# The experts' sum takes in the residual on TensorE, and the last norm reads PSUM

## The chip, the cores and the metric

One core of a Trainium2 chip runs the whole program in one launch. The metric is the device time of that launch in microseconds (us), the median of several runs. Everything is float32; products on TensorE (PE) are either full float32, which the trace shows as two passes per product, or products of rounded halves (fp32r) in one pass each.

## The reference, cut to what matters

Two blocks of two layers each work on 256 tokens of 1024 columns. The change is in the second block, at the end of each of its layers: the experts' output is added to the residual `h`, and after the last layer comes a last norm.

```python
def expert_choice_ffn(xn, w_router, w_gate, w_up, w_down):
    aff = softmax(xn @ w_router)                      # 256 x 16
    g, idx = top_k(aff.T, 32)                         # 32 tokens for each of 16 experts
    xs = xn[idx]
    hid = silu(xs @ w_gate[e]) * (xs @ w_up[e])
    y = (hid @ w_down[e]) * g
    return zeros_like(xn).at[idx].add(y)

for l in range(2):
    xn = rms_norm_2(h, attn_norm[l])
    ...                                               # three kinds of attention
    h = h + o @ w_out[l]
    h = h + expert_choice_ffn(rms_norm_2(h, ffn_norm[l]), ...)
return rms_norm_2(h, final_norm)                      # x * rsqrt(mean(x*x) + eps) * gain
```

## The kernel before, in words

Each engine has a function of its own (`tensor`, `vector`, `scalar`, `pool`, `sync`), and the program is what these functions issue in the order in which they are written. Nothing is scheduled: what orders engines among each other are semaphores, counted by name (`P("scat", l, q)` is PE's count, `V` VectorE's, `A` ScalarE's, `G` GpSimd's, `D` the DMAs').

The residual `x` has 128 partitions and two halves `t` of tokens by two halves `h` of columns, so four tiles of 128x512, numbered n = 2t + h. `xG` is a copy of it that ScalarE makes before the experts (`x_apart`), with the columns in another order: column 4q + c lies at c * 128 + q, so that weights loaded from it lie side by side. Who reads it back in the order of `x` steps over 512 bytes from one value to the next. The place of `x` itself is then used for expert weights.

`experts(l)` in each engine's function runs 18 stages. In stage s PE makes gate and up of expert s (`gate_up`), adds the output of expert s - 2 to the sum over experts (`scatter`: four products of 128x512, one for each tile n, which gather over all 16 experts in four PSUM banks called "moe"), makes the down product of expert s - 1 (`down`) and turns the hidden values (`hidden`). In stage 2 there is also `rest`: 16 gather products and 32 transposes, after which the four banks are taken and `scatter(0)` follows. PE's `scatter` goes through the tiles in the order n = 0, 2, 1, 3. Banks of PSUM are taken in turn, and PE waits for the last reader of a bank when it takes it.

Expert weights come in blocks of 2 MB, in the order of use, over 16 DMA engines. SyncE (SP) issues a block when its place is free, that is, when PE has read the block before it in that place, and it issues strictly in order.

After stage 17, VectorE adds `xG` to each bank and writes `x` (`x_out`, four additions). In layer 0 the next layer follows: PE transposes `x` (`turn`), ScalarE rounds the first weights (`w_high`, tile r, then wp) and the transposed values (`h_high_b`, tile hp), VectorE makes their remainders (`w_low`, `h_low_b`). In layer 1 ScalarE squares and sums the four tiles of `x`, VectorE and GpSimd make the root for each half t (`root_of`, `root`), VectorE multiplies with root and gain (`result`), and SP stores each half t.

Of the kernel before, what the change touches and what calls it, by code (L numbers as in the profile page):

```python
# [301 lines left out]
def program(nc, a, c1off, c2off, out):  # L302
    ctx = ExitStack()
    with ctx:

        def v4(ap, *d):
            s = " ".join("abcdef"[:len(d) + 1])
            kw = {"abcdef"[i]: d[i] for i in range(len(d))}
            return ap.rearrange("p (" + s + ") -> p " + s, **kw)
# [107 lines left out]
        def ps(*key):  # L417
            return banks[psum.at.get(key, 0)]
# [280 lines left out]

        def tensor(e):

            def mm(o, l, r, start=True, stop=True):
                return e.matmul(o, l, r, start=start, stop=stop)  # L705
# [75 lines left out]
            def turn(site, l, of, cps=range(4)):  # L781

                ks = []
                spare(l, "turn", site)
                for cp in cps:
                    if cp % 2 == 0:
                        for t in range(2):
                            e.wait_ge(*((A if cp else V)("normed", site, l, t) if of is None else V("x", *of, 2 * t + cp // 2)))
                    k, pb = bank("turn", site, l, cp)
                    for j in range(2):  # L790
                        for t in range(2):
                            cc = 2 * cp + j
                            m = tr(pb[:, 256 * j + 128 * t:256 * j + 128 * t + 128],
                                   xn[:, 1024 * t + 128 * cc:1024 * t + 128 * cc + 128] if of is None else
                                   x4[:, t, cc // 4, :, cc % 4] if site == "fn" else x3[:, t, 128 * cc:128 * cc + 128])
                    m.then_inc(*P.up("turn", site, l, cp))
                    ks.append(k)
                return ks
# [697 lines left out]
            def experts(l):  # L1496
# [106 lines left out]
                def scatter(q):  # L1603
                    if q == 0:
                        e.wait_ge(*V("PW", l, 6))
                        e.wait_ge(*A("PW", l, 7))
                    for hf in range(2):
                        e.wait_ge(*(A if hf else V)("Y", l, q))
                        for t in range(2):
                            m = mm(acc[2 * t + hf][1][:, :], PW[:, q, 128 * t:128 * t + 128], Ys[q % 2][:, hf, :], q == 0, q == 15)  # L1610
                            if hf and t:
                                m.then_inc(*P.up("scat", l, q))
                            elif q == 15:
                                m.then_inc(*P.up("scat_part", l, hf, t))
                acc = []
                for s in range(18):
                    if s < 16:
                        gate_up(s)
                    if s > 2:
                        scatter(s - 2)  # L1620
                    if 1 <= s <= 16:
                        down(s - 1)
                    if s < 16:
                        hidden(s)
                    if s == 2:
                        rest()
                        acc += [bank("moe", l, n) for n in range(4)]
                        scatter(0)
                for n in range(4):
                    psum.until(acc[n][0], V, "x", "moe", l, n)  # L1630

            condition()
            for l in range(2):
# [6 lines left out]
        def vector(e):  # L1640
# [13 lines left out]
            def stt(o, i0, s, i1, op0, op1):  # L1654
                own()
                return e.scalar_tensor_tensor(out=o, in0=i0, scalar=s, in1=i1, op0=op0, op1=op1)  # L1656
# [388 lines left out]
                e.wait_ge(*P(name, l, 0))  # L2045
                copy(dst[:, 0:512], ps(name, l, 0)[:, :]).then_inc(*V.up(name, l, 0))

            def x_out(site, l, gB, after=None):
                for t, h in ((t, h) for h in range(2) for t in range(2)):
                    n = 2 * t + h  # L2050
                    xs_ = x3[:, t, 512 * h:512 * h + 512]
                    pb = ps(*(("moe", l, n) if site == "moe" else ("mlp2", l, n) if site == "mlp" else ("acc", site, l, n)))
                    e.wait_ge(*((P("scat", l, 15) if n == 3 else P("scat_part", l, h, t)) if site == "moe" else P("acc", site, l, n)))
                    if gB is not None:
                        tmp = xn[:, 0:512]
                        tt(tmp, pb[:, :], gB[:, 512 * h:512 * h + 512], ALU.mult).then_inc(*V.up("x_", site, l, n))
                        tt(xs_, xs_, tmp, ALU.add).then_inc(*V.up("x", site, l, n))
                    else:
                        apart = xG[:, t, h].rearrange("p c q -> p q c")
                        tt(v4(xs_, 128), apart, v4(pb[:, :], 128), ALU.add).then_inc(*V.up("x", site, l, n))  # L2060
                    if after is not None:
                        after(n)

            def cut(l, g):
                if l == 0 and g == 16:
# [264 lines left out]
            def experts(l):  # L2330
# [68 lines left out]
                for s in range(17):  # L2399
# [3 lines left out]
                        hidden(s)  # L2403
                    if s == 2:
                        rest()
                x_out("moe", l, None, last if l else None)

            def root_of(t):
                e.wait_ge(*A("sq", "moe", 1, 2 * t + 1))
                tt(S("ss", 2)[:, t:t + 1], sq4[:, 2 * t:2 * t + 1], sq4[:, 2 * t + 1:2 * t + 2], ALU.add).then_inc(*step())  # L2410
                ts(rstd[:, t:t + 1], S("ss", 2)[:, t:t + 1], EPS, None, ALU.add).then_inc(*V.up("root", "last", t))

            def result(t):
                e.wait_ge(*G("root", "last", t))
                stt(xn[:, 1024 * t:1024 * t + 1024], x3[:, t, :], rstd[:, t:t + 1], fg, ALU.mult, ALU.mult).then_inc(*V.up("out", t))

            def last(n):

                if n == 3:
                    root_of(0)  # L2420
                    e.wait_ge(*D("fg"))
                    root_of(1)
                    result(0)
                    result(1)

            params()
            for l in range(2):
# [6 lines left out]
        def scalar(e):  # L2434
# [35 lines left out]
            def square(site, l, t, h, junk, wait=True):  # L2470
                n = 2 * t + h
                if wait:
                    e.wait_ge(*V("x", site, l, n))
                act(junk, x3[:, t, 512 * h:512 * h + 512], ACT.Square, scale=1.0 / 32, accum=sq4[:, n:n + 1]).then_inc(*A.up("sq", site, l, n))

            def squares(site, l, wait=True, some=range(4)):
                for i in some:
                    t, h = i % 2, i // 2
                    square(site, l, t, h, sqr_end if site == "moe" else sqr, wait)
# [428 lines left out]
            def experts(l):  # L2908
# [41 lines left out]
                    if s == 2:  # L2950
                        rest()
                if l:
                    squares("moe", l)

            params()
            for l in range(2):
# [47 lines left out]
        def sync(e):  # L3004
# [58 lines left out]
                            e.dma_start(raw[64 * (r % 2):64 * (r % 2) + 64, r // 2, h], src).then_inc(*D.up("rpb", l))  # L3063
            for t in range(2):
                e.wait_ge(*V("out", t))
                e.dma_start(out[0][128 * t:128 * t + 128, :], xn[:, 1024 * t:1024 * t + 1024]).then_inc(*D.up("out"))
            e.wait_ge(*D("out"))

# [39 lines left out]
```

## Time and profile before

| | |
|---|---|
| time, median of 3 runs | 2180.13 us |
| all runs | 2179.51, 2180.13, 2181.79 us |
| span of the profiled execution | 2178.9 us |
| PE busy | 1867.2 us, 86% |
| VectorE busy | 910.8 us, 42% |
| ScalarE busy | 643.5 us, 30% |
| share of the chain that ended last | PE 60%, DMA 27%, DVE 9%, ACT 2% |
| HBM read | 614.44 MB |

The profile's page gives the span of the profiled execution, from its first to its last instruction, and no other time of it. Busy shares are means over a program with very different stages: most of it is bound by PE, but the two experts' stages read their weights as fast as the DMA engines bring them. DVE is VectorE, ACT ScalarE, PEld the weight load of PE, SPq the queue of SyncE.

### The profile page before, as it was taken

To read this page: it belongs to the slowest core of one execution; us is meant where nothing else is said; L and a number is where in the kernel's file an instruction comes from. 1 tells how busy PE (TensorE), PEld (TensorE's weight loads), DVE (VectorE), ACT (ScalarE), POOL (GpSimd) and SP (SyncE) were. 2 spreads that over 40 slices of the span, in tenths; PEclk is the share of its full clock that TensorE was granted. 3 is DMA by queue.
4 is the path that set the end of the run, shared out by engine and by line. 5 is a ranking of instruction groups with operands and counts; after the bars stand their busy time and mean duration, and the time that the engine had idled before them with its cause. 6 is when DMAs were issued, how large, how long until landed. Compare 5 with 4: busy or idle time off the path is not lost.

```text
span 2178.9 us, 31064 instructions
## 1 busy us (share of the span) xinstructions
PE 1867.2 (86%) x12856; PEld 1237.8 (57%) x12856; DVE 910.8 (42%) x1514; ACT 643.5 (30%) x1110; POOL 43.2 (2%) x46
## 2 busy tenths in 40 slices
PE   6999999999999999999899866666798997666666
PEld 3887888987888889988654321122275542121212
DVE  3675576655576576645762200000068530000002
ACT  3244235535244235534452100000045410000001
POOL 0001000000002000000000000000000000000000
PEclk9999999999999999999999988887899998888888
DMA  9565348556534345453659999999983799999997
GB/s 334 219 232 194 118 155 309 194 187 215 217 116 156 117 155 179 170 194 88 253 195 373 429 426 427 427 427 427 421 269 137 307 395 426 427 427 427 427 425 316
DMA packets 119750, 617.50 MB, mean 283 GB/s; under 512 B 18448, under 2 KB 21434, under 8 KB 86586
## 3 DMA queue, kind: packets, MB, share of 16 engines
q1 hardware_dynamic: 119034, 613.85, 71.2%
q8 instruction: 103, 1.69, 0.3%
q10 hardware_dynamic: 576, 1.66, 0.2%
q14 instruction: 37, 0.30, 0.0%
HBM read 614.44 MB, written 1.05 MB: 282 GB/s over the span
## 4 chain that ended last, share of the span: by engine, by line
PE 60%; DMA 27%; DVE 9%; ACT 2%; issue 1%; SPq 0%; POOL 0%; DVEq 0%; ACTq 0%
PE pb L705 57%; DMA ring<-in_w_up_dram 18%; DMA ar<-in_w_up_dram 4%; DMA x<-in_w_up_dram 3%; PE pb L708 3%; DVE ar L1648 2%; DVE ar L1656 1%; DMA ring<-in_w_down_dram 1%; DMA ring<-in_ada_w_dram 1%; DVE small L1664 1%; DVE ar L1652 1%; ACT ar L2447 1%; DVE ar L1660 1%; DVE x L1648 1%; DVE small L1652 0%
## 5 line engine op out<-in xcount | busy, mean ns | idle before, releaser
L705 PE MATMUL pb<-ring,ar 128*32 128x512 f32 (+2 forms) x2144 | 402.0, 724 | 185.4 <-DMA ring<-in_w_up_dram 103.1
L705 PE MATMUL pb<-ar 64*64 64x64 f32 (+10 forms) x3680 | 418.7, 348 | 34.2 <-DMA ring<-in_w_up_dram 27.0
L2451 ACT COPY ar<-pb 128x512 f32<-128x512 f32 (+2 forms) x195 | 112.6, 578 | 910.5 <-PE pb L705 852.5
L1660 DVE COPY ar<-pb 128x512 f32<-128x512 f32 (+3 forms) x94 | 57.5, 611 | 723.1 <-PE pb L705 713.2
L705 PEld LDWEIGHTS pb<-ring,ar 128*32 128x32 f32 (+1 forms) x2144 | 104.5, 132 | 395.6 <-issue 379.5
L705 PEld LDWEIGHTS pb<-ar 64*64 64x64 f32 (+5 forms) x3680 | 218.5, 147 | 186.2 <-issue 162.5
L705 PE MATMUL pb<-hT,ring 128*128 128x256 f32 x1024 | 235.4, 386 | 0.4 <-ACT ar L2447 0.4
L705 PEld LDWEIGHTS pb<-hT,ring 128*128 128x128 f32 x1024 | 193.0, 192 | 33.6 <-issue 7.8
L1648 DVE TENSOR_TENSOR ws<-ring,ws 128x1024 fp32r<-128x1024 f32 x128 | 156.9, 1226 | 124.2 <-ACT ws L2451 122.4
L705 PE MATMUL pb<-hs,ws 128*128 128x256 f32 x1536 | 187.1, 284 | 2.7 <-ACT aux L2451 1.4
L705 PEld LDWEIGHTS pb<-hs,ws 128*128 128x128 f32 x1536 | 185.7, 193 | 4.5 <-ACT aux L2451 1.6
L705 PE MATMUL pb<-ws,h1s 128*128 128x512 f32 x768 | 175.7, 390 | 0.0
L2451 ACT CAST ws<-ring 128x1024 fp32r<-128x1024 f32 x128 | 134.2, 1048 | 127.5 <-PE pb L705 123.7
L705 PEld LDWEIGHTS pb<-ws,h1s 128*128 128x128 f32 x768 | 144.0, 188 | 30.8 <-issue 1.0
L705 PE MATMUL pb<-wp,hp 128*128 128x512 f32 (+1 forms) x636 | 141.0, 381 | 3.3 <-DVE wp L1648 1.6
L705 PEld LDWEIGHTS pb<-wp,hp 128*128 128x128 f32 x636 | 114.8, 190 | 28.2 <-DVE wp L1648 3.9
L708 PEld LDWEIGHTS pb<-c,ar 128*128 128x128 f32 (+3 forms) x620 | 73.6, 155 | 67.2 <-issue 40.6
L708 PE MATMUL pb<-c,ar 128*128 128x128 f32 (+3 forms) x620 | 91.0, 284 | 24.0 <-DMA c<-in_c_dram 9.0
L705 PE MATMUL pb<-hT,ar 128*32 128x512 f32 x200 | 67.5, 809 | 36.4 <-DMA ring<-in_w_up_dram 36.4
L1648 DVE TENSOR_TENSOR wp<-ring,wp 128x1024 fp32r<-128x1024 f32 (+1 forms) x53 | 61.2, 1155 | 55.8 <-ACT wp L2451 54.3
L2451 ACT CAST wp<-ring 128x1024 fp32r<-128x1024 f32 (+1 forms) x53 | 52.5, 991 | 55.8 <-PE pb L705 54.8
L1656 DVE SCALAR_TENSOR_TENSOR ar<-ar,pb 128x256 f32<-128x256 f32 (+1 forms) x84 | 40.7, 485 | 65.2 <-ACT ar L2447 58.1
(175 smaller groups left out, 1655.2 us busy)
## 6 DMA issues: line engine op xcount, KB each, us to landing
ring<-in_w_down_dram SPq DMA_DIRECT2D x46, 2048.0 KB, 28.0
ring<-in_w_gate_dram SPq DMA_DIRECT2D x42, 2048.0 KB, 28.6
ring<-in_w_up_dram SPq DMA_DIRECT2D x42, 2048.0 KB, 23.6
ring<-in_w_mlp_dram SPq DMA_DIRECT2D x32, 2048.0 KB, 7.8
ring<-in_w_in_dram SPq DMA_DIRECT2D x27, 2048.0 KB, 9.0
ring<-in_ada_w_dram SPq DMA_DIRECT2D x24, 2048.0 KB, 8.4
ar<-in_w_gate_dram SPq DMA_DIRECT2D x12, 2048.0 KB, 28.0
ar<-in_w_up_dram SPq DMA_DIRECT2D x12, 2048.0 KB, 23.0
```

What stands on the lines that cost most here:

```text
L705: return e.matmul(o, l, r, start=start, stop=stop)
L708: return e.transpose(o, i, ident[0:i.shape[0], 0:i.shape[0]])
L1648: return e.tensor_tensor(o, i0, i1, op)
L1652: return e.tensor_scalar(o, i, s1, s2, op0, op1)
L1656: return e.scalar_tensor_tensor(out=o, in0=i0, scalar=s, in1=i1, op0=op0, op1=op1)
L1660: return e.tensor_copy(o, i)
L1664: return e.tensor_reduce(o, i, AX.X, op)
L2447: return e.activation(o, i, fn, scale=scale, **kw)
L2451: return e.copy(o, i)
```

## The change

PE starts each "moe" bank with a product of the unit matrix and the tile of `xG`, so that the bank holds residual plus experts when `scatter(15)` is done; the first expert's product now adds to it. At the end of layer 0 VectorE copies the tiles n = 0 and 2 to `x`, ScalarE n = 1 and 3. At the end of layer 1 nothing is written to `x`: ScalarE squares each bank, VectorE multiplies the bank with the gain `fg` after that, and the multiplication with the root is left for the end, with columns 0 to 511 of each half t on VectorE and 512 to 1023 on ScalarE.

```diff
+        def x_by(site, n):
+            return A if site == "moe" and n % 2 else V
...
                         for t in range(2):
-                            m = mm(acc[2 * t + hf][1][:, :], PW[:, q, 128 * t:128 * t + 128], Ys[q % 2][:, hf, :], q == 0, q == 15)
+                            m = mm(acc[2 * t + hf][1][:, :], PW[:, q, 128 * t:128 * t + 128], Ys[q % 2][:, hf, :], False, q == 15)
...
                     if s == 2:
                         rest()
-                        acc += [bank("moe", l, n) for n in range(4)]
+                        for n in range(4):
+                            acc.append(bank("moe", l, n))
+                            mm(v4(acc[n][1][:, :], 128), ident, xG[:, n // 2, n % 2].rearrange("p c q -> p q c"), True, False)
                         scatter(0)
...
# vector, in x_out (the case of "moe" goes)
-                    else:
-                        apart = xG[:, t, h].rearrange("p c q -> p q c")
-                        tt(v4(xs_, 128), apart, v4(pb[:, :], 128), ALU.add).then_inc(*V.up("x", site, l, n))
...
-                x_out("moe", l, None, last if l else None)
+                if l:
+                    last()
+                else:
+                    for t in range(2):
+                        e.wait_ge(*P("scat_part", l, 0, t))
+                        copy(x3[:, t, 0:512], ps("moe", l, 2 * t)[:, :]).then_inc(*V.up("x", "moe", l, 2 * t))
...
-            def result(t):
-                e.wait_ge(*G("root", "last", t))
-                stt(xn[:, 1024 * t:1024 * t + 1024], x3[:, t, :], rstd[:, t:t + 1], fg, ALU.mult, ALU.mult).then_inc(*V.up("out", t))
...
+            def last():
+                e.wait_ge(*D("fg"))
+                for n in (0, 2, 1, 3):
+                    t, h = divmod(n, 2)
+                    e.wait_ge(*A("sq", "moe", 1, n))
+                    if h:
+                        root_of(t)
+                    at = xn[:, 1024 * t + 512 * h:1024 * t + 512 * h + 512]
+                    tt(at, ps("moe", 1, n)[:, :], fg[:, 512 * h:512 * h + 512], ALU.mult).then_inc(*V.up("gained", n))
+                for t in range(2):
+                    e.wait_ge(*G("root", "last", t))
+                    half = xn[:, 1024 * t:1024 * t + 512]
+                    ts(half, half, rstd[:, t:t + 1], None, ALU.mult).then_inc(*V.up("out", t))
...
# scalar, experts
                 if l:
-                    squares("moe", l)
+                    last()
+                else:
+                    for t in range(2):
+                        e.wait_ge(*(P("scat", l, 15) if t else P("scat_part", l, 1, t)))
+                        copy(x3[:, t, 512:1024], ps("moe", l, 2 * t + 1)[:, :]).then_inc(*A.up("x", "moe", l, 2 * t + 1))
+            def last():
+                for n in (0, 2, 1, 3):
+                    t, h = divmod(n, 2)
+                    e.wait_ge(*(P("scat", 1, 15) if n == 3 else P("scat_part", 1, h, t)))
+                    act(sqr_end, ps("moe", 1, n)[:, :], ACT.Square, scale=1.0 / 32, accum=sq4[:, n:n + 1]).then_inc(*A.up("sq", "moe", 1, n))
+                for t in range(2):
+                    e.wait_ge(*G("root", "last", t))
+                    e.wait_ge(*V("gained", 2 * t + 1))
+                    half = xn[:, 1024 * t + 512:1024 * t + 1024]
+                    act(half, half, ACT.Copy, scale=rstd[:, t:t + 1]).then_inc(*A.up("out", t))
```

PE's program in stage 2 of the experts of layer 0, before. The row of 32 is the transposes of `rest`, `pb<-ar 128x512 x4` is `scatter(0)`, and the 16 rows of 32x512 with the rows after them are `gate_up(3)` (c is the tile with constants, which holds the unit matrix).

```order
1129 L708 MATMUL pb<-c,ar 128x128 x32
1130 L705 MATMUL pb<-ar 128x512 x4
1131 L705 MATMUL pb<-ring,ar 32x512 x16
1132 L705 MATMUL pb<-hT,ar 32x512 x2
1133 L705 MATMUL pb<-ring,ar 32x512 x2
```

And the same place of the changed kernel:

```order
1129 L712 MATMUL pb<-c,ar 128x128 x32
1130 L709 MATMUL pb<-ar,c 128x512 x4
1131 L709 MATMUL pb<-ar 128x512 x4
1132 L709 MATMUL pb<-ring,ar 32x512 x16
1133 L709 MATMUL pb<-hT,ar 32x512 x2
```

Four products stand ahead of `scatter(0)`, and so ahead of everything that PE reads from the ring of weights from there on; layer 1 has the same.

ScalarE's program from the last output of the experts of layer 0 into layer 1, before:

```order
400 L2451 COPY ar<-pb 128x512
401 L2451 CAST r<-ring 128x1024
402 L2447 ACTIVATE hp<-pb,late 128x256 x4
403 L2451 CAST wp_0<-ring 128x1024
404 L2447 ACTIVATE hp<-pb,late 128x256 x4
```

The changed kernel at this place:

```order
400 L2458 COPY ar<-pb 128x512
401 L2458 COPY x<-pb 128x512 x2
402 L2458 CAST r<-ring 128x1024
403 L2454 ACTIVATE hp<-pb,late 128x256 x4
404 L2458 CAST wp_0<-ring 128x1024
405 L2454 ACTIVATE hp<-pb,late 128x256 x4
```

The first rounding of weights of layer 1 (CAST r) now stands behind two copies that wait for PE's last products.

VectorE's last rows, before and then of the changed kernel:

```order
1004 L1648 TENSOR_TENSOR x<-ar,pb 128x512 x4
1005 L1648 TENSOR_TENSOR small<-sq 128x1
1006 L1652 TENSOR_SCALAR rstd<-small 128x1
1007 L1648 TENSOR_TENSOR small<-sq 128x1
1008 L1652 TENSOR_SCALAR rstd<-small 128x1
1009 L1656 SCALAR_TENSOR_TENSOR xn<-x,rstd,ar 128x1024 x2
```

```order
1004 L1654 TENSOR_TENSOR xn<-pb,ar 128x512 x2
1005 L1654 TENSOR_TENSOR small<-sq 128x1
1006 L1658 TENSOR_SCALAR rstd<-small 128x1
1007 L1654 TENSOR_TENSOR xn<-pb,ar 128x512
1008 L1654 TENSOR_TENSOR small<-sq 128x1
1009 L1658 TENSOR_SCALAR rstd<-small 128x1
1010 L1654 TENSOR_TENSOR xn<-pb,ar 128x512
1011 L1658 TENSOR_SCALAR xn<-xn,rstd 128x512 x2
```

The additions are gone, the product with the gain is ahead of the root, and two short multiplications are left behind it.

## Rows read from the trace of the kernel before

**Rows 1.** The page's first line.

```profile
span 2178.9 us, 31064 instructions
```

**Rows 2.** Windows over the experts of layers 0 and 1: busy, PEclk, DMA share, GB/s.

```profile
1166.00:1582.00 416.00, 296.50 (x1748) 96.99 (x1752) 35.28 (x67) 30.04 (x58) 0.00 (x0) 0.85 1.01 426
...
1748.00:2160.00 412.00, 283.48 (x1715) 94.06 (x1716) 34.84 (x66) 30.35 (x59) 0.00 (x0) 0.86 1.01 426
```

**Rows 3.** Chain that ended last, 1582 to 1600: start, us, what.

```profile
1583.98 1.06 DVE x L1648
...
1587.46 1.04 DVE x L1648
...
1588.59 1.24 DVE r L1648
...
1596.97 3.25 PE pb L705 x13
```

**Rows 4.** Timeline at the end of layer 0: start, us, engine, line, operation.

```profile
1582.81 3.70 PE L705 MATMUL pb<-ar 128*128 128x512 f32 x8
...
1584.50 1.04 ACT L2451 CAST r<-ring 128x1024 fp32r<-128x1024 f32 x1 [0.92 <-DMA ring<-in_w_in_dram]
...
1586.99 2.06 ACT L2447 ACTIVATE hp<-pb,late 128x256 fp32r<-128x256 f32 x4 [1.45 <-PE pb L708]
```

**Rows 5.** Chain that ended last, from 2166 to the end.

```profile
2167.72 1.05 DVE x L1648
...
2173.04 0.17 DVE small L1648
...
2173.23 0.16 DVE rstd L1652
...
2174.90 1.28 DVE xn L1656
```

**Rows 6.** Timeline of the end of layer 1.

```profile
2166.55 3.70 PE L705 MATMUL pb<-ar 128*128 128x512 f32 x8
...
2168.80 0.63 ACT L2447 ACTIVATE ar<-x 128x512 f32<-128x512 f32 x1 [1.47 <-DVE x L1648]
...
2169.33 0.19 ACT L2447 ACTIVATION_READ_ACCUMULATOR ar<-x 128x1 f32 x1
```

**Rows 7.** DMA issues from 2170 on: count, KB each, us to landing.

```profile
out_dram<-xn SPq DMA_DIRECT2D x2, 512.0 KB, 2.7
```

**Rows 8.** Groups by form, whole program: busy us, mean ns, idle before.

```profile
L2451 ACT COPY ar<-pb 128x512 f32<-128x512 f32 x181 | 106.0, 586 | 900.3 <-PE pb L705 849.4 <-PE pb L708 45.9
L1660 DVE COPY ar<-pb 128x512 f32<-128x512 f32 x64 | 44.2, 691 | 717.7 <-PE pb L705 710.1 <-PE pb L708 4.6 <-DVE ar L1648 0.5
...
L1648 DVE TENSOR_TENSOR xn<-pb,ar 128x512 f32<-128x512 f32 x8 | 5.5, 691 | 9.6 <-PE pb L705 9.6
...
L2447 ACT ACTIVATE xn<-x,rstd 128x512 f32<-128x512 f32 x8 | 5.8, 722 | 5.0 <-POOL rstd L2972 4.8
...
L1652 DVE TENSOR_SCALAR xn<-x,rstd 128x512 f32<-128x512 f32 x8 | 3.9, 486 | 3.4 <-POOL rstd L2972 3.2
```

**Rows 9.** Timeline of PE at `scatter(0)`, layer 0.

```profile
1209.24 3.67 PE L705 MATMUL pb<-ar 128*128 128x512 f32 x8 [0.87 <-ACT ar L2451]
```

**Rows 10.** DMA issues in three moments (1163.6, 1216.5, 1798.9 us), as rows 7.

```profile
ring<-in_w_gate_dram SPq DMA_DIRECT2D x1, 2048.0 KB, 8.3
...
ring<-in_w_up_dram SPq DMA_DIRECT2D x1, 2048.0 KB, 9.8
...
ring<-in_w_up_dram SPq DMA_DIRECT2D x1, 2048.0 KB, 10.4
```

**Rows 11.** Windows of L708 (transposes) alone: PE busy, PEld busy, PEclk, DMA.

```profile
1144.00:1146.20 2.20, 1.20 (x8) 1.11 (x8) 1.00 0.94 402
1586.00:1588.00 2.00, 1.04 (x8) 0.89 (x8) 1.00 1.06 391
```

**Rows 12.** ScalarE's reads of x in `x_apart`, layer 0: min/median/max ns.

```profile
L2447 ACT ACTIVATE ar<-x x4: 1108/1114/1123, 1147.3 to 1152.9; 128x512 f32<-128x512 f32 x4
```

More of the change, by code:

```diff
@@ L787, in turn @@
                         for t in range(2):
-                            e.wait_ge(*((A if cp else V)("normed", site, l, t) if of is None else V("x", *of, 2 * t + cp // 2)))
+                            e.wait_ge(*((A if cp else V)("normed", site, l, t) if of is None else x_by(of[0], cp // 2)("x", *of, 2 * t + cp // 2)))
                     k, pb = bank("turn", site, l, cp)
@@ L1626, in experts @@
                         rest()
-                        acc += [bank("moe", l, n) for n in range(4)]
+                        for n in range(4):
+                            acc.append(bank("moe", l, n))
+                            mm(v4(acc[n][1][:, :], 128), ident, xG[:, n // 2, n % 2].rearrange("p c q -> p q c"), True, False)
                         scatter(0)
-                for n in range(4):
-                    psum.until(acc[n][0], V, "x", "moe", l, n)
+                for n in range(4 if l == 0 else 0):
+                    psum.until(acc[n][0], x_by("moe", n), "x", "moe", l, n)
             condition()
@@ L2046, in spread, with x_out @@
                 copy(dst[:, 0:512], ps(name, l, 0)[:, :]).then_inc(*V.up(name, l, 0))
-            def x_out(site, l, gB, after=None):
+            def x_out(site, l, gB):
                 for t, h in ((t, h) for h in range(2) for t in range(2)):
@@ L2051, in x_out @@
                     xs_ = x3[:, t, 512 * h:512 * h + 512]
[L2052 to L2057, printed above, removed]
-                    else:
-                        apart = xG[:, t, h].rearrange("p c q -> p q c")
-                        tt(v4(xs_, 128), apart, v4(pb[:, :], 128), ALU.add).then_inc(*V.up("x", site, l, n))
-                    if after is not None:
-                        after(n)
+                    pb = ps(*(("mlp2", l, n) if site == "mlp" else ("acc", site, l, n)))
+                    e.wait_ge(*P("acc", site, l, n))
+                    tmp = xn[:, 0:512]
+                    tt(tmp, pb[:, :], gB[:, 512 * h:512 * h + 512], ALU.mult).then_inc(*V.up("x_", site, l, n))
+                    tt(xs_, xs_, tmp, ALU.add).then_inc(*V.up("x", site, l, n))
             def cut(l, g):
@@ L2411, in root_of @@
                 ts(rstd[:, t:t + 1], S("ss", 2)[:, t:t + 1], EPS, None, ALU.add).then_inc(*V.up("root", "last", t))
-            def result(t):
-                e.wait_ge(*G("root", "last", t))
-                stt(xn[:, 1024 * t:1024 * t + 1024], x3[:, t, :], rstd[:, t:t + 1], fg, ALU.mult, ALU.mult).then_inc(*V.up("out", t))
[L2417 to L2424, printed above, removed]
+            def last():
[11 more added lines that the diff above has]
+                    ts(half, half, rstd[:, t:t + 1], None, ALU.mult).then_inc(*V.up("out", t))
             params()
@@ L2472, in square @@
                 if wait:
-                    e.wait_ge(*V("x", site, l, n))
+                    e.wait_ge(*x_by(site, n)("x", site, l, n))
                 act(junk, x3[:, t, 512 * h:512 * h + 512], ACT.Square, scale=1.0 / 32, accum=sq4[:, n:n + 1]).then_inc(*A.up("sq", site, l, n))
@@ L3065, in sync @@
                 e.wait_ge(*V("out", t))
+                e.wait_ge(*A("out", t))
                 e.dma_start(out[0][128 * t:128 * t + 128, :], xn[:, 1024 * t:1024 * t + 1024]).then_inc(*D.up("out"))
```

## The prediction

> **What bounds the kernel now.** I read the stages first, because the page's shares are means over stages with different limits. In the experts of both layers the DMA engines are busy all the time, a share of 1.01 at 426 GB/s, while PE has 296 of 416 us and 283 of 412 us of work at a clock of 0.85 [rows 2]. There PE's work costs nothing as long as it doesn't hold back an issue of weights until the engines run dry. The chain of waits then shows the two places where the changed lines are on the path. Between the layers it runs through VectorE: four additions from 1583.98 to 1588.50, the remainder of the first weights at 1588.59, and so on without a gap until PE takes over at 1596.97 [rows 3]. At the end it runs through the same four additions from 2167.72 on, the sums and roots, and the last product, which ends at 2176.18 [rows 5]; the store lands 2.7 us later [rows 7], which makes the span of 2178.9 [rows 1].
>
> **The end of layer 1.** PE's last eight passes start at 2166.55 and take 3.70 [rows 6], 0.86 us between tiles, and the first addition starts at 2167.72 [rows 5]. So tiles are ready at 2167.72, 2168.58, 2169.44 and 2170.30, while the additions take 1.05 each and fall behind PE. In the changed kernel ScalarE squares each tile at once. A square with the read of its sum takes 0.72 us (2168.80 to 2169.52) [rows 6], less than 0.86, so ScalarE keeps PE's pace and is done at 2171.02. VectorE waits for each square, then multiplies, 0.69 each [rows 8]. Its third product ends at about 2171.3, the second pair of small operations takes 0.17 + 0.16 and gaps [rows 5] to 2171.65, the last product ends at 2172.4. The first root has come from GpSimd by then. Two multiplications of 0.49 [rows 8] end at 2172.9 and 2173.5; ScalarE's second half starts at 2172.5 and takes 0.72 [rows 8], to 2173.2, hidden beside it. The last store is issued at 2173.5 instead of 2176.2: 2.7 us earlier. But the stores were 1.3 us apart and are now 0.5 apart. A half of 512 KB is 1.2 us of the engines at 426 GB/s, so the second may queue for 0.7 us. The gain is 2.0 to 2.7; I take 2.3.
>
> **Between the layers.** VectorE now copies two tiles of 0.69 [rows 8] and is free at 1585.5, 3 us earlier. That isn't passed on, since its next operation needs ScalarE's first rounded weights. ScalarE made these at 1584.50 to 1585.54, while it had nothing else to do until 1586.99 [rows 4]. They now stand behind two copies of 0.59 [rows 8], of which the second waits for the last product: 1582.81 + 3.70 = 1586.51, so copy from 1586.65 to 1587.25, rounding to 1588.3. VectorE's remainder starts at 1588.35 instead of 1588.59, a gain of 0.24 of the 3. Queued behind the copies on ScalarE are the eight roundings of hp, which begin at 1588.35 instead of 1586.99. Each pair of them takes 1.03 [rows 4], so the first is ready at 1589.4, before VectorE asks for it at 1589.6, and the second at 1590.4, before 1590.7. VectorE stays the one that PE waits for, and 0.2 us is won. If ScalarE's lateness of 1.3 us were on the path I would lose up to 1.1, so the range of this term is +1.1 to -0.24.
>
> **The four products of the unit matrix, in each layer.** The nearest row is `scatter(0)` itself: eight passes in 3.67 us [rows 9]. PE is idle for 0.87 ahead of it, for ScalarE's last copy [rows 9]; the new products don't need this copy and fill that gap. The banks are those of the first four transposes' outputs, read out long before. So `gate_up(3)` and all issues behind it come later by d = 3.67 - 0.87 = 2.8 us, if a pass costs the same. It may not: the streamed operand steps by 512 bytes, and no row of before shows a streamed operand with such a step. Three rows show what steps cost. PE's transposes load `x` with a step of 16 bytes in one place and side by side in another: eight take 1.20 against 1.04 of PE, and 1.11 against 0.89 of weight load [rows 11]. VectorE's addition with the step of 512 bytes takes 1.06 [rows 3], against 0.69 for the same form without it [rows 8]. ScalarE's copies of `x` with 16 bytes take 1.11 [rows 12] against 0.59 [rows 8]. So the four products cost between 3.67 (no loss) and 3.67 x 1.11/0.59 = 6.9 us. I take the row of the same engine, 3.67 x 1.20/1.04 = 4.2; with the ratio of loads it would be 4.6. Then d is 3.4, between 2.8 and 6.0.
>
> The Trainium skill speaks against this change here. "SBUF — State Buffer", under "Door 1: The DMA port swizzle", has lines of 16 bytes in SBUF, of which each one newly entered costs extra, so that an fp32 stream that steps over more than four values pays at every value. The rows of VectorE and ScalarE agree; PE's load pays less than they do. By that rule the cost would be nearer to 6.9.
>
> **What d costs.** How much can the issues slip before the engines run dry? The block issued at 1216.5 landed 9.8 us later, in layer 1 the one at 1798.9 after 10.4 us, both behind older blocks; one issued into an empty queue at 1163.6 landed after 8.3 [rows 10]. That leaves 1.5 and 2.1 us. But a start from rest is ragged, and the bare size says less: the store of 512 KB lands after 2.7 [rows 7], and 2 MB are 3.7 us more at 426 GB/s, so 6.4, and leaves 3.4 and 4.0. I take the middle, 2.4 and 3.0. With d = 3.4 the stream loses 1.0 in layer 0 and 0.4 in layer 1. As the share stays at 1.01 up to the end [rows 2], what it loses reaches the end whole: +1.4. The bounds are 0 (d = 2.8 with the wide margins) and (6.0 - 1.5) + (6.0 - 2.1) = +8.4.
>
> **Sum.** -2.3 - 0.2 + 1.4 = -1.1 us, a span of 2177.8. The median of the runs shown, 2180.13, is 1.2 above the profiled span of 2178.9, so 2179.0 us. What a measurement of this kernel can tell from no change is about 0.2%, 4.4 us.
>
> **Rivals.**
> *The stream doesn't notice (0.30).* If the wide margins are right, d = 3.4 costs nothing and the whole of 2.5 us is kept: 2177.6. For it speaks that PE has slack of a third in the stage; against it the landing of 8.3.
> *Steps cost PE what they cost the others (0.27).* One place decides: the four products at 6.9 us, by the ratio of ScalarE's rows, and the first issue behind them. With d = 6.0 the losses are 3.6 + 3.0 by the middle margins, 6.6 less 2.5: 2184.2, slower by 0.19%; by the narrow margins 8.4 less 2.5, 2186.0. The time is above that of before from a loss of 2.5 on, which is d = 3.95, or products of 4.8 us. For it: two engines of three read at about 1.75 ns a value with steps. Against it: PE's own load in rows 11, and that a full float32 pass streams slowly anyhow, 0.46 us for 512 values. The Trainium skill's rule above is this rival.
> *The boundary gives more (0.05).* VectorE is free 3 us earlier; if PE could use all of that, -2.3 - 3.0 with no loss would be 2174.8, faster by 0.24%. Against it stands the rounding that now waits on ScalarE [rows 4].
> *ScalarE becomes the bound between the layers (0.08).* The eight roundings of hp start 1.3 us later; with 1.1 lost instead of 0.2 won, 2180.3.
> My forecast itself has 0.30.
>
> **How the numbers follow.** The predicted time is that of the forecast, 2179.0; its own range is 2177.5 to 2181, from the terms' bounds short of the rivals. The range of 2176.8 to 2185.0 leaves out the boundary that gives more, a tenth below that is noise, and the narrow-margin end of the second rival. Chances: faster by over 0.2% needs 2175.8 or less, the third rival and little else, 0.05; slower needs 2184.5 or more, the upper half of the second rival, 0.14; the rest, 0.81, is within 0.2%.
>
> **What would show it.** In the changed profile, (1) the products of c and ar ahead of `scatter(0)`: 3.7, 4.2 or 6.9 us for eight passes, starting right behind the transposes; (2) the landing of the first block issued behind them, 8.3 or less would mean an empty queue, and a window around it a DMA share below 1.00; (3) VectorE's remainder at 1588.35 on the clock of before, after taking out what the stream lost; (4) from PE's last pass to the issue of the last store 3.2 us where it was 5.9, and the landing of the second store at 2.7 or up to 3.4. The prediction is wrong if the streamed passes double, or if ScalarE's squares from PSUM take over 0.86 us and so fall behind PE.

## The result, and the profile after

The changed kernel takes 2191.3 us (median of 4 runs, 2190.11 to 2192.15), the kernel before beside it 2180.96. The ratio is 1.0046, interval 1.0033 to 1.0058: slower, by about 10 us, and outside the forecast range of 2176.8 to 2185.0. Its profiled span is 11.2 us longer than that of [rows 1]:

```profile
span 2190.1 us, 31096 instructions
```

PE at the first expert, layer 0, of the changed kernel (start, us, engine, line, operation). L709 is the line of the products, which was L705; the first row, `pb<-c,ar` of L712, is the transposes of `rest`, and `pb<-ar,c` are the products of the unit matrix with `xG`:

```profile
1206.18 3.66 PE L712 MATMUL pb<-c,ar 128*128 128x128 f32 x32
1209.67 7.13 PE L709 MATMUL pb<-ar,c 128*128 128x512 f32 x8
1216.62 3.61 PE L709 MATMUL pb<-ar 128*128 128x512 f32 x8
```

The eight passes take 7.13 us where the eight of `scatter(0)` behind them, of the same size, take 3.61. Without the wait of 0.87 [rows 9], `scatter(0)` comes 6.95 - 0.87 = 6.1 us later than it would.

The windows around this place show what that does to the weights (columns: length, busy time of PE, PEld, DVE, ACT, POOL, then TensorE's clock, the DMA share and GB/s). The changed kernel:

```profile
1216.00:1219.00 3.00, 3.00 (x7) 1.15 (x6) 0.00 (x0) 0.00 (x0) 0.00 (x0) 1.00 1.01 431
1219.00:1222.00 3.00, 3.00 (x23) 0.83 (x25) 0.00 (x0) 0.00 (x0) 0.00 (x0) 1.00 0.67 284
1222.00:1225.00 3.00, 3.00 (x36) 0.91 (x32) 0.00 (x0) 0.00 (x0) 0.00 (x0) 1.00 0.25 44
1225.00:1228.00 3.00, 3.00 (x26) 0.92 (x19) 0.00 (x0) 0.58 (x1) 0.00 (x0) 1.00 0.84 306
```

The kernel before, at the same block:

```profile
1213.00:1216.00 3.00, 3.00 (x32) 0.91 (x28) 0.00 (x0) 0.00 (x0) 0.00 (x0) 1.00 0.99 421
1216.00:1219.00 3.00, 3.00 (x36) 0.91 (x28) 0.00 (x0) 0.00 (x0) 0.00 (x0) 1.00 0.97 415
1219.00:1222.00 3.00, 3.00 (x17) 1.06 (x7) 0.00 (x0) 0.58 (x1) 0.00 (x0) 1.00 1.00 421
```

PE is busy throughout, the DMA engines are not: in nine microseconds they miss (0.33 + 0.75 + 0.16) x 3 = 3.7 us of transfer. In layer 1 the matching windows, from 1809 us on, read 0.33, 0.43 and 0.92, which is 4.0 us. The first block issued behind `scatter(0)` now lands about as fast as into an empty queue (8.3 in [rows 10]); DMA issues of the changed kernel at 1223.9 and at 1812.9 us, as rows 7:

```profile
ring<-in_w_up_dram SPq DMA_DIRECT2D x1, 2048.0 KB, 8.8
...
ring<-in_w_up_dram SPq DMA_DIRECT2D x1, 2048.0 KB, 8.3
```

The end of layer 0 in the changed kernel, which answers to [rows 3, 4]. Lines of ACT, DVE and PE in order of time:

```profile
1588.93 3.70 PE L709 MATMUL pb<-ar 128*128 128x512 f32 x8
...
1590.95 0.69 DVE L1666 COPY x<-pb 128x512 f32<-128x512 f32 x1 [0.17 <-PE pb L709]
1591.81 0.58 ACT L2458 COPY x<-pb 128x512 f32<-128x512 f32 x1 [2.11 <-PE pb L709]
1592.67 0.59 ACT L2458 COPY x<-pb 128x512 f32<-128x512 f32 x1 [0.27 <-PE pb L709]
1593.34 1.05 ACT L2458 CAST r<-ring 128x1024 fp32r<-128x1024 f32 x1
1594.42 1.23 DVE L1654 TENSOR_TENSOR r<-ring,r 128x1024 fp32r<-128x1024 f32 x1 [2.77 <-ACT r L2458]
1594.48 2.06 ACT L2454 ACTIVATE hp<-pb,late 128x256 fp32r<-128x256 f32 x4
1595.61 2.77 PE L709 MATMUL pb<-r,hp 128*128 128x512 f32 x11 [1.19 <-ACT hp L2454]
```

From the last group of PE to VectorE's remainder it is 5.49 us; it was 5.78 [rows 3, 4]. VectorE is idle for 2.77 in front of it, for ScalarE's rounding. PE's own first product of layer 1 comes no sooner for this: it waits 1.19 us for ScalarE's `hp` and starts 6.68 us after the last group. In the kernel before it was 6.60, from 1582.81 [rows 4] to this row:

```profile
1589.41 2.99 PE L705 MATMUL pb<-r,hp 128*128 128x512 f32 x12
```

PE is ahead only from the next weights on, by 0.27 us.

The end of the program in the changed kernel, which answers to [rows 5, 6]:

```profile
2179.22 3.70 PE L709 MATMUL pb<-ar 128*128 128x512 f32 x8
...
2180.39 0.60 ACT L2454 ACTIVATE ar<-pb 128x512 f32<-128x512 f32 x1 [0.48 <-PE pb L709]
...
2180.88 0.19 ACT L2454 ACTIVATION_READ_ACCUMULATOR ar<-pb 128x1 f32 x1
...
2181.16 1.49 DVE L1654 TENSOR_TENSOR xn<-pb,ar 128x512 f32<-128x512 f32 x2 [1.99 <-ACT ar L2454]
2181.24 0.60 ACT L2454 ACTIVATE ar<-pb 128x512 f32<-128x512 f32 x1 [0.17 <-PE pb L709]
...
2182.60 0.19 ACT L2454 ACTIVATION_READ_ACCUMULATOR ar<-pb 128x1 f32 x1
...
2183.25 0.16 DVE L1654 TENSOR_TENSOR small<-sq 128x1 f32<-128x1 f32 x1 [0.59 <-ACT ar L2454]
...
2184.84 0.69 DVE L1654 TENSOR_TENSOR xn<-pb,ar 128x512 f32<-128x512 f32 x1
...
2185.64 1.08 DVE L1658 TENSOR_SCALAR xn<-xn,rstd 128x512 f32<-128x512 f32 x2
2186.15 0.95 SPq L3090 DMA_DIRECT2D out_dram<-xn  x2
```

And the landing of its last store, issued behind 2186.7 (DMA issues, as rows 7):

```profile
out_dram<-xn SPq DMA_DIRECT2D x1, 512.0 KB, 3.4
```

From the start of PE's last group to the end of the span it was 2178.9 - 2166.55 = 12.35 us [rows 1, 6] and is now 10.88.

**Where 11.2 us went.** I split both timelines at the starts of `scatter(0)` and of the last scatter in each layer, and count the new products' delay of 6.08 us with the stage that it holds up. The stage of layer 0 is then 4.8 us longer, that of layer 1 4.7, what lies between them 1.9, the end 1.5 shorter; 1.3 us come from ahead of the experts of layer 0, in code that is the same in both. In sum 11.2. The small terms are rough, since two profiles of one kernel differ by as much: `scatter(0)` of layer 0 starts at 1209.24 us in the first profile of the kernel before and at 1211.85 in the second.

The 1.9 between the stages is nearly all TensorE's clock. The new end of layer 0 gives -0.3; then come -1.6 where the clock of before falls and that of the changed kernel doesn't, and +3.95 here. Windows of the changed kernel in layer 1 (columns as above):

```profile
1735.00:1740.00 5.00, 3.83 (x16) 2.94 (x16) 2.52 (x11) 3.66 (x8) 0.00 (x0) 0.65 0.98 416
1740.00:1745.00 5.00, 4.71 (x16) 3.51 (x16) 2.50 (x10) 0.76 (x1) 0.00 (x0) 0.50 0.65 218
1745.00:1750.00 5.00, 5.00 (x20) 4.55 (x19) 1.08 (x3) 0.00 (x0) 0.00 (x0) 0.50 0.49 208
```

A granted clock of 0.50 is the level of 1.2 GHz. The experiments come back to it, since this loss didn't stay in a second profile of the same kernel.

### The profile page after: what moved, and what is told of

Same layout as the page of the kernel before. It is cut to its first block, busy times and chain, and to the rows that moved or that the text cites. A ratio compares the mean times of both kernels' runs of the same rounds, so it can differ in the third digit from the quotient of the medians.

```text
span 2190.1 us, 31096 instructions
## 1 busy us (share of the span) xinstructions
PE 1889.6 (86%) x12872; PEld 1245.0 (57%) x12872; DVE 905.5 (41%) x1512; ACT 646.0 (29%) x1114; POOL 43.2 (2%) x46
## 4 chain that ended last, share of the span: by engine, by line
PE 59%; DMA 26%; DVE 10%; ACT 3%; issue 1%; SPq 0%; POOL 0%; DVEq 0%; ACTq 0%
PE pb L709 56%; DMA ring<-in_w_up_dram 17%; DMA ar<-in_w_up_dram 4%; DMA x<-in_w_up_dram 3%; PE pb L712 2%; DVE ar L1654 2%; DVE ar L1662 2%; DVE small L1670 1%; DVE ar L1658 1%; DMA ring<-in_ada_w_dram 1%; ACT ar L2454 1%; DVE ar L1666 1%; DVE small L1658 0%; DVE xn L1654 0%; ACT hp L2454 0%
## 5 line engine op out<-in xcount | busy, mean ns | idle before, releaser
L709 PE MATMUL pb<-ring,ar 128*32 128x512 f32 (+2 forms) x2144 | 407.4, 734 | 177.7 <-DMA ring<-in_w_up_dram 100.4
L709 PE MATMUL pb<-ar 64*64 64x64 f32 (+10 forms) x3680 | 419.4, 348 | 32.5 <-DMA ring<-in_w_up_dram 27.3
L709 PEld LDWEIGHTS pb<-ring,ar 128*32 128x32 f32 (+1 forms) x2144 | 105.4, 133 | 390.9 <-issue 377.7
L709 PEld LDWEIGHTS pb<-ar 64*64 64x64 f32 (+5 forms) x3680 | 220.4, 147 | 186.5 <-issue 165.7
L709 PE MATMUL pb<-hT,ring 128*128 128x256 f32 x1024 | 235.4, 386 | 0.4 <-ACT ar L2454 0.4
L709 PEld LDWEIGHTS pb<-hT,ring 128*128 128x128 f32 x1024 | 193.0, 192 | 33.6 <-issue 7.8
L709 PE MATMUL pb<-hs,ws 128*128 128x256 f32 x1536 | 186.0, 283 | 3.7 <-ACT aux L2458 1.4
L709 PEld LDWEIGHTS pb<-hs,ws 128*128 128x128 f32 x1536 | 184.7, 192 | 5.5 <-ACT aux L2458 1.7
L709 PE MATMUL pb<-ws,h1s 128*128 128x512 f32 x768 | 175.7, 390 | 0.0
L709 PEld LDWEIGHTS pb<-ws,h1s 128*128 128x128 f32 x768 | 144.0, 188 | 30.8 <-issue 1.0
L709 PE MATMUL pb<-wp,hp 128*128 128x512 f32 (+1 forms) x636 | 139.9, 378 | 3.3 <-ACT wp L2458 1.6
L709 PEld LDWEIGHTS pb<-wp,hp 128*128 128x128 f32 x636 | 113.6, 188 | 28.3 <-DVE wp L1654 4.0
L712 PEld LDWEIGHTS pb<-c,ar 128*128 128x128 f32 (+3 forms) x620 | 73.3, 154 | 65.7 <-issue 39.5
L712 PE MATMUL pb<-c,ar 128*128 128x128 f32 (+3 forms) x620 | 90.7, 283 | 22.4 <-DMA c<-in_c_dram 8.9
L709 PE MATMUL pb<-hT,ar 128*32 128x512 f32 x200 | 65.6, 788 | 36.1 <-DMA ring<-in_w_up_dram 36.1
```

Of the source, the lines that this page charges most:

```text
L712: return e.transpose(o, i, ident[0:i.shape[0], 0:i.shape[0]])
```

## The experiments

Theory A: the step of 512 bytes in the streamed operand doubles a pass, and the products stand where the weights have no slack. Rivals: the place alone, whatever a pass costs; the copies at the end of layer 0; the new products themselves, wherever they stand.

**Side by side.** The products without the step (edit of the changed kernel; the residual's columns end up in another order).

```diff
-mm(v4(acc[n][1][:, :], 128), ident, xG[:, n // 2, n % 2].rearrange("p c q -> p q c"), True, False)
+mm(v4(acc[n][1][:, :], 4), ident, xG[:, n // 2, n % 2], True, False)
```

> The changed kernel, but the four unit products stream each tile of xG as it lies, side by side, without the step of 512 bytes; the residual's columns are then added in a wrong order. Theory (stepped stream, dry engines): the eight passes take 3.7 us instead of 7.1, the issues behind them slip by 2.8 instead of 5.9, the engines lose about 1.3 and 0.7 us in the two layers instead of 4.6 and 4.5, and the time falls by some 7 us to 2184, or 2181 if the half clock at 1735 to 1750 us goes as well. Rival (any work of PE at this place costs its whole time, steps or not): the passes fall to 3.7, and about 3 us per layer stay lost, 2186 or more. Rival (the half clock before the experts of layer 1 is what the change costs): it stays, and the time hardly moves, 2190.

Measured: 2183.05 us (10 runs), ratio to before 1.0009 (1.0000 to 1.0018). PE in its trace, with the same columns as above:

```profile
1207.88 3.60 PE L709 MATMUL pb<-ar,c 128*128 128x512 f32 x8
1211.31 3.60 PE L709 MATMUL pb<-ar 128*128 128x512 f32 x8
```

The same product, bank, place and count costs 3.60 instead of 7.13. The step is 3.5 us of each group, and most of the loss goes with it.

**Products later.** The four products hidden one at a time in stages 6 to 9, with the step; `scatter(0)` starts the banks.

```diff
-    mm(v4(acc[n][1][:, :], 128), ident, xG[...].rearrange("p c q -> p q c"), True, False)
...
+    if 6 <= s < 10:
+        n = s - 6
+        mm(v4(acc[n][1][:, :], 128), ident, xG[...].rearrange("p c q -> p q c"), False, False)
```

> The changed kernel, with the four unit products not ahead of scatter(0) but one each behind the hidden step of stages 6 to 9, where PE waits for weights; same sums in another order. Theory: each product still takes 1.8 us, but the landing of blocks there is 20 us and more, so no issue that matters slips; the 9.1 us of the two layers come back, and the gains of the end (1.5) and of the boundary (0.3) are left: 2179 against 2181 of before. Rival (the four stepped products disturb wherever they stand): 2185 or more.

Measured: 2178.05 us (10), ratio 0.9991 (0.9982 to 1.0000). The landings of the first block behind `scatter(0)` are 10.0 and 10.4 us again. The same slow passes cost nothing where PE has slack: what hurts is the place times the size.

**No residual.** The four products are left out, and so the residual is missing from the output.

> The changed kernel without the unit products; the residual is left out of the sum after the experts. Theory: the same time as with the products in stages 6 to 9, 2179, and the first block issued in stage 3 lands after 9.8 to 10.4 us again. Rival (the rest of the change, copies on ScalarE and the new end, costs too): above 2181.

Measured: 2177.99 us (10), ratio 0.9986 (0.9976 to 0.9995). That is the time of the version above: products in stages 6 to 9 are free within what this can tell.

**Before and unit.** The kernel before, with the four products ahead of `scatter(0)` and nothing else changed (the residual is then added twice).

```diff
+for n in range(4):
+    acc.append(bank("moe", l, n))
+    mm(v4(acc[n][1][:, :], 128), ident, xG[...].rearrange("p c q -> p q c"), True, False)
```

> The kernel before with nothing but the four unit products ahead of scatter(0); VectorE still adds xG at the end, so the residual counts twice. Theory: all of the loss and none of the gain, 2181 + 9.1 = 2190, and 2194 if the half clock ahead of layer 1's experts comes with it. Rival (the loss is in the copies, the end or the clock): within 2 us of 2181.

Measured: 2189.55 us (5), ratio 1.0039 (1.0026 to 1.0052), 8.5 us slower than before. PE in its trace:

```profile
1208.03 7.13 PE L705 MATMUL pb<-ar,c 128*128 128x512 f32 x8
...
1795.73 7.13 PE L705 MATMUL pb<-ar,c 128*128 128x512 f32 x8
```

The products alone make the loss; the new ends aren't needed for it.

**Changed again.** The changed kernel once more.

> The changed kernel itself, timed beside its parts on one chip. The unit products in the kernel before cost 8.5 us (2189.6 against 2181.1), and the rest of the change wins 3.1 (2178.0 against 2181.1), so the two together should give 2186.5. The first timing gave 2191.3. Theory (the parts add up, the rest is chance from one time to the next): 2186 to 2188. Rival (the parts meet: TensorE's half clock between 1735 and 1750 us, which the kernel before and the one with the unit products alone don't show, comes with the whole change): 2190 or more again, with the half clock in its profile.

Measured: 2189.94 us (4), ratio 1.0042 (1.0028 to 1.0056), before beside it 2180.14. So the loss is there again. The time is nearer to the rival's 2190 than to the 2186 to 2188 of the theory that the parts add up, but the half clock that the rival wanted with it cost only 1.6 us in this profile. The parts measured apart, 1.0039 and 0.9991, make 1.0030, and their intervals are wide enough to reach 1.0042: whether the parts meet is not shown.

**Round first.** Products in stages 6 to 9, and at the end of layer 0 ScalarE's first rounding of weights ahead of its two copies.

```diff
             def block2(l):
-                if l:
-                    w_high("b", l, 0)
...
                 if l:
                     last()
                 else:
+                    w_high("b", 1, 0)
                     for t in range(2):
```

> Unit products in stages 6 to 9, and on ScalarE the first rounding of layer 1's weights ahead of the two copies of x. Theory (VectorE's 3 us aren't passed on because its next operand is rounded late): the rounding ends at about 1585.5 on the clock of before, VectorE's remainder follows its copies at once, at 1585.6 instead of 1588.35, the roundings of hp start at 1587.3, and PE takes over 1 to 2 us earlier: 2176 to 2177 against 2178.1 with the rounding behind. Rival (ScalarE or PE's transposes set the pace anyhow): no difference, 2178.

Measured: 2177.6 us (12), ratio 0.9989 (0.998 to 0.9997). Its trace at the end of layer 0 (last group of PE, rounding, remainder, first product of layer 1):

```profile
1581.78 3.70 PE L709 MATMUL pb<-ar 128*128 128x512 f32 x8
...
1583.39 1.04 ACT L2460 CAST r<-ring 128x1024 fp32r<-128x1024 f32 x1 [0.92 <-DMA ring<-in_w_in_dram]
...
1584.59 1.23 DVE L1656 TENSOR_TENSOR r<-ring,r 128x1024 fp32r<-128x1024 f32 x1
...
1587.32 2.96 PE L709 MATMUL pb<-r,hp 128*128 128x512 f32 x12
```

From the last group to the products of layer 1 it is 5.5 us, where it is 6.7 in the changed kernel. Further on, the same products of layer 1 start 1.3 us sooner after the last group than in the version without this edit. So the rounding behind the copies did hold this place, as forecast. The whole time can't tell this version from the one with the products in stages 6 to 9 alone.

**The ends apart.** One with only the end of layer 1 changed, one with only the end of layer 0, both with the products of that layer in stages 6 to 9.

> Only the end of layer 1 is changed (unit products of layer 1 in stages 6 to 9); layer 0 ends with VectorE's four additions as before. Theory: it wins 1.5 us at the end, 2179.5; from PE's last pass to the second store's issue 3.8 us, its landing 3.4. If the half clock at 1730 to 1750 comes from the boundary's other timing, it isn't there. Rival (it comes by chance of the execution): it may be.

> Only the end of layer 0 is changed (copies on VectorE and ScalarE, unit products of layer 0 in stages 6 to 9); the end of layer 1 is as before. Theory: 0.3 us won at the boundary and nothing else, 2180.8, with VectorE's remainder 5.5 us after the first pass of the last scatter instead of 5.8. With the theory of the half clock from the boundary it is in this profile. Rival (the boundary wins more further down, as the chain of the changed kernel was 1.6 us shorter between 1672 and 1704): 2179.

Measured: 2179.41 us (10), ratio 0.9996 (0.9988 to 1.0005), and 2180.17 us (10), ratio 0.9999 (0.9988 to 1.0010). Neither is told from before by its time, but the traces are finer: from the last group of PE to the end of the span is 10.8 us with the changed end. With the old end it is 12.4 in three profiles; the 12.7 of the version with only layer 0 changed has a pause of 0.47 us between VectorE's additions that the others haven't. Layer 0's end gains 0.29 to the remainder and, further on, 0.22 to 0.25 for PE.

**One and two of the products there.** The other three or two in stages 6 to 9, to see how much delay the weights bear.

```diff
+    if n < 1:      # 2 in the second version
         mm(v4(acc[n][1][:, :], 128), ident, xG[...].rearrange("p c q -> p q c"), True, False)
```

> The changed kernel with the unit product of tile n = 0 alone ahead of scatter(0), and those of n = 1, 2, 3 in stages 7 to 9. Theory (each layer's weights lose what PE's delay d exceeds a margin of about 1.3 us, worked out from the runs so far): two passes take 1.8 us, d = 1.8 - 0.87 = 0.9, below the margin, so the stage of either layer from the first scatter to the last is 374.1 less 0.9 = 373.2 in layer 0 and about 374.0 in layer 1, nothing is lost, and the time is that of all four in stages 6 to 9, 2178 +- 1.5. Rival (each us of delay is lost, there is no margin): 0.9 lost in each layer, so 374.1 and 374.9 stay, and the time is 2180.

> The changed kernel with the unit products of n = 0 and 1 ahead of scatter(0), and those of n = 2 and 3 in stages 8 and 9. Four passes with the step take 3.6 us, as eight did side by side. Theory (the delay counts, not the step): d = 2.7, the same as with four products side by side, so 1.4 lost in each layer and a time of 2181 +- 1.5 (that run: 2183.05). Rival (the step itself disturbs the stream, by what it does to the memory that DMA writes to): more than with four side by side, over 2184.

Measured: 2181.47 us (11), ratio 0.9998 (0.9990 to 1.0007), and 2182.67 us (11), ratio 1.0005 (0.9996 to 1.0014). The first was to take 2178, so that forecast was 3.5 too low; the second lies just above its 2181 +- 1.5. PE with one product there, and with two:

```profile
1211.49 1.90 PE L709 MATMUL pb<-ar,c 128*128 128x512 f32 x2
```

```profile
1208.13 3.65 PE L709 MATMUL pb<-ar,c 128*128 128x512 f32 x4
```

The table takes the stage of each layer from the start of `scatter(0)` to that of the last scatter, out of the timelines, adds the delay d of the products, and subtracts the median of the eight profiles without products there (374.2 us in layer 0, 374.7 in layer 1; they spread over 373.6 to 374.5 and 374.4 to 375.6).

| products ahead of `scatter(0)` | d | lost, layer 0 | lost, layer 1 |
|---|---|---|---|
| one, with the step | 0.85 | 0.9 | 1.4 |
| four, side by side | 2.6 | 1.7 | 1.3 |
| two, with the step | 2.6 | 1.3 | 1.4 |
| four, before and unit | 6.1 | 4.8 | 4.6 |
| four, changed kernel | 6.1 | 4.2 | 4.9 |
| four, changed again | 6.1 | 5.0 | 4.9 |

At equal d, two products with the step lose what four without it lose, within the spread: the delay counts and not the step. Above 2.6 us a microsecond of delay costs about one. The single product was to cost nothing by my theory of a margin of 1.3 us, and its row reads 0.9 and 1.4. The profiles without products spread by up to 0.6 us about their median in layer 0 and 0.9 in layer 1, so these rows can't say whether the margin is a soft one or smaller than 1.3.

**Before again, and round first again.** Second profiles of both.

> The kernel before, unchanged, for a second profile. Theory (where TensorE's clock is granted at half in layer 1 goes by how much work stands where ahead of it, so by the end of layer 0): half at 1685 to 1690 again and not at 1735 to 1750. Rival (chance of the execution): at another place, or not at all.

> The kernel with the unit products in stages 6 to 9 and ScalarE's first rounding ahead of its two copies, unchanged, for a second profile and more times. Theory: the ratio is 0.9989 again within its interval (0.998 to 0.9997), the end of layer 0 is passed 1.3 us faster than without the rounding first, and TensorE has its full clock from 1685 to 1690. Whether it is granted half at 1730 to 1750 differs between executions of one program, if the difference between the two profiles of the changed kernel (6.8 and 1.7 us of lost clock there) is chance: then it may appear here too, and cost up to 4 us.

Measured: 2183.56 us (1 run, too few to compare), and 2177.93 us (12), ratio 0.9988 (0.9978 to 0.9997). Windows of before's second profile, and of the other's:

```profile
1688.00:1693.00 5.00, 4.37 (x22) 2.57 (x24) 4.16 (x10) 2.56 (x8) 0.00 (x0) 0.66 0.00 0
...
1735.00:1740.00 5.00, 3.83 (x13) 2.82 (x12) 3.23 (x14) 4.21 (x7) 0.00 (x0) 0.71 0.84 357
```

```profile
1688.00:1693.00 5.00, 5.00 (x30) 2.93 (x30) 4.01 (x13) 2.54 (x8) 0.00 (x0) 1.00 0.29 52
...
1735.00:1740.00 5.00, 3.95 (x14) 3.40 (x15) 1.91 (x7) 0.00 (x0) 0.00 (x0) 0.63 0.86 308
1740.00:1745.00 5.00, 5.00 (x34) 3.89 (x36) 1.70 (x3) 0.00 (x0) 0.00 (x0) 0.68 0.27 113
```

With 14 profiles the clock in layer 1 can be read against the end of layer 0. In the four with the old end (before twice, before and unit, the end of layer 1 alone) the clock falls to half for some microseconds at about 105 us after the last scatter, and what lies between the two experts' stages takes 208.7 to 208.9 us (without d). In the ten with the new end it doesn't fall there, which is worth 1.64 us each time. But in these ten a later fall, about 150 us after the last scatter, costs between 0 and 4.05 us (in order of size 0, 0, 0.1, 0.2, 1.6, 3.1, 3.2, 3.2, 3.95, 4.05). In the four it costs nothing, though it isn't absent there: the clock falls at this place in before's second profile (0.71 above) and in that of the end of layer 1 alone (0.75 in the same window), and the stretch takes 208.8 and 208.9 us all the same. So of the theory for before's second profile the fall at 105 us came true, and the full clock further on did not. The changed kernel lost 3.95 in one profile and 1.6 in the other, round first 0 and 3.2: so the size of the second loss is chance of the execution. The mean of the ten is 1.9, as much as the 0.25 of the new end and the 1.64 together. So the new end of layer 0 wins 0.25 us in its own place and, in the mean of these profiles, nothing in the whole, which agrees with its own run (0.9999).

## Why the prediction was wrong, step by step

**The four products: the step that failed.** I took 4.2 us, the ratio of PE's own transposes in [rows 11]; they took 7.13, just above the upper bound of 6.9 that ScalarE's rows gave. The side by side run shows that the step of the streamed operand is the whole of the difference. My row was the wrong one of the same engine: the transposes stream the unit matrix and load `x` as weights, so their step is on the other input. I argued against the second rival that a full float32 pass streams slowly anyhow, 0.46 us for 512 values; the stepped pass took 0.89, so a pass that is slow anyhow didn't hide the step. And my figure for the other two engines, about 1.75 ns a value, was too low for their rows: 1.06 and 1.11 us for 512 values are 2.1 and 2.2. It is PE's stepped pass that comes to 1.74. The Trainium skill's rule ("SBUF — State Buffer", "Door 1: The DMA port swizzle") spoke for the dear price, and this trace agrees: 0.89 against 0.45 us a pass.

**What d costs: narrow margins, not the middle.** d = 6.1 was the second rival's 6.0. It lost 4.8 and 4.7 us, so 1.3 and 1.4 us of it were borne, against margins taken as 2.4 and 3.0, and against the narrow ones of 1.5 and 2.1 from the landings. The landing of a full block into an empty queue was the nearer row; the store of 512 KB, by which I widened the margins, led away. But one profile can't give the margin to a microsecond: in the eight profiles without products there, the same block of layer 0 landed after 9.6 to 11.0 us and that of layer 1 after 9.6 to 10.7 (before's second profile: 11.0 and 10.0), so the same reading gives anything from 1.3 to 2.7. "Reaches the end whole" was right: the share of 1.01 can't win anything back. In place of +1.4 stands +9.5. It is above the bound of 8.4 mostly because the margins were smaller than even the narrow ones, 0.2 and 0.7 us; the delay itself was only 0.08 us above the bound's 6.0 in each layer.

**The end of layer 1: right in kind, 0.8 too much.** Forecast -2.3, measured -1.5 (12.4 to 10.9, in all profiles with this end within 0.1). ScalarE kept PE's pace, one square each 0.86 us. But VectorE's root operation started at 2183.25, 0.46 after ScalarE had read the sum of tile n = 1 at 2182.60 + 0.19 = 2182.79, where I had let it follow at once. With small gaps behind it, this makes the last store's issue 0.55 later than in my sum. What it waits for isn't shown: it is no general price of passing a result, since VectorE's first product started 0.09 after ScalarE's read (2181.07 to 2181.16), and so did the second root operation of the kernel before (2172.95 to 2173.04). The last store was issued about 2.1 us earlier, and landed in 3.4, not 2.7, the far end of what the sum had allowed for a queue behind the first; this is the rest of the 0.8.

**Between the layers: right.** Forecast -0.2 with VectorE waiting for the rounding; measured -0.29 to the remainder in all eight profiles that have this end as it stands. But PE's first product of layer 1 waits for ScalarE's `hp` and starts 0.08 later than before; VectorE is what PE waits for only from the next weights on. Round first shows that the copies held the rounding, and gives another 1.3 us at this place. What the sum had no term for is the clock of layer 1, -1.6 and then 0 to +4.05.

**The sum, made again** with measured terms: -1.5 - 0.25 + 9.5, and for the clock -1.6 + 1.9 in the mean, is +8 us. The two comparisons say +10.3 and +9.8, with intervals from 7.2 to 12.7 and 6.1 to 12.2. The sum lies within both; of the 2 us between it and the medians no run shows a place.

**The rivals.** The second one, "steps cost PE what they cost the others", was what happened. Its 2184.2 to 2186.0 lay 4.1 to 5.9 us above the kernel before, and the run 10.3: it was short by the margins, the end's 0.8 and what the sum above leaves open. I gave it 0.27 and let the range end inside it. The others fell: the stream did notice; the boundary gave 0.25 and not 3; and ScalarE's lateness between the layers, though PE waits for it once, lost none of the 1.1.

**A version that beats both.** Products in stages 6 to 9 with the rounding first: 0.9989 (0.998 to 0.9997) and 0.9988 (0.9978 to 0.9997) against before, about 2.5 us faster in both comparisons.

## What to carry to other kernels

A transfer-bound stage with a third of PE idle still has places without slack. Before putting work there, look up when the next block behind it is issued, and compare its landing with that of a block into an empty queue: the difference is a rough upper bound of what may be added. Take it from several profiles. Here it read 1.3 to 2.7 us, about 1.3 of a delay of 6.1 was borne, and even a delay of 0.85 may not have been free. The same work four stages later cost nothing.

To price an operand with a step, take the row where the same input of the same engine has one. If there is none, take the dearest row of any engine into the range at least: here it gave 6.9 for a measured 7.13, and the row of the right engine but the wrong input gave 4.2.

## What the hardware showed unexpectedly

A full float32 pass of 128x512 on PE takes 0.45 us with the streamed operand side by side and 0.89 us with a step of 512 bytes between values, for 7.13 against 3.60 us for eight. ScalarE and VectorE pay in like measure, 1.11 against 0.59 us [rows 8, 12] and 1.06 against 0.69 [rows 3, 8]. So all three read a tile with such steps (16 or 512 bytes) at about 1.7 to 2.2 ns a value.

TensorE's granted clock in layer 1 went with the end of layer 0, though that end shifts PE by only 0.25 us. In the four profiles with the old end PE was idle for 1.06 to 1.09 us for VectorE's `ar`, and after four transposes for 0.63 or 0.64, ahead of the fall to 0.66 of a window of 5 us; in the ten with the new end the first of these was 0.42 or 0.43, the second the same, and the clock stayed. Whether this gap decides it wasn't tried. The later fall, about 150 us after the last scatter, cost 3.95 and 1.6 us in two executions of one program and 0 and 3.2 in two of another, so a single profile can't price an edit that stands ahead of such a place.
